# The first block's input projection as three split products, with the gates kept in DRAM

## The reference, cut to what matters

```python
x = layer_norm(x, ln_emb_g, ln_emb_b)
z = x @ w_in                                             # 1024 x 2048, with kr twice
xs, gs, cq, ckv, kr, gm = split(z)                       # 512, 512, 256, 128, 64, 512
ys = s5_branch(xs, ...) * silu(gs)                       # state-space scan, GELU, GLU
ym = mla_branch(cq, ckv, kr, ...) * silu(gm)             # latent attention, 4 heads
mix = concat([ys, ym]) @ w_out
```

## Time and profile before

| | |
|---|---|
| median of 3 runs | 2280.45 us (2280.33 to 2280.82) |
| profiled execution, first to last instruction | 2278.5 us |
| PE busy | 2194.5 us (96%) |
| DVE busy | 1154.4 us (51%) |
| POOL busy | 1192.3 us (52%) |
| ACT busy | 754.5 us (33%) |
| input projection and what lies between its tiles | 36.3 to 285.75 us |

### The profile page before, as it was taken

The page is one execution under the profiler, slowest core; times in us unless marked ns, Lnnn a source line. Parts: engine busy times, 40 slices in busy tenths (PEclk is TensorE's granted clock), DMA queues, the critical chain, the costliest instruction groups (busy, mean ns, idle before and its releaser), DMA issues.

```text
span 2278.5 us, 27616 instructions
## 1 busy us (share of the span) xinstructions
PE 2194.5 (96%) x10944; PEld 1609.4 (71%) x10944; DVE 1154.4 (51%) x1473; ACT 754.5 (33%) x1161; POOL 1192.3 (52%) x809
## 2 busy tenths in 40 slices
PE   6999999999999899999999999998999999999998
PEld 2454464676886687568866788876788888888886
DVE  6950844551186611550036724775966666652434
ACT  4121042332112511650036343135555555531211
POOL 2533510204787265435656765365688888844442
PEclk8999999999999999999999999999999999999999
DMA  3336232001223422101211235233122222154111
GB/s 134 111 74 104 84 85 70 4 19 47 92 84 98 143 65 84 34 10 37 89 25 51 83 111 194 87 144 130 47 62 82 83 82 84 64 182 157 47 37 74
DMA packets 62590, 187.73 MB, mean 82 GB/s; under 512 B 14903, under 2 KB 17255, under 8 KB 62415
## 3 DMA queue, kind: packets, MB, share of 16 engines
q1 hardware_dynamic: 50688, 143.30, 19.6%
q10 hardware_dynamic: 8688, 32.26, 3.8%
q0 software_dynamic: 3088, 10.43, 2.4%
HBM read 150.15 MB, written 33.59 MB: 81 GB/s over the span
## 4 chain that ended last, share of the span: by engine, by line
PE 89%; DVE 5%; ACT 3%; issue 2%; POOL 1%; DMA 1%; ACTq 0%; DVEq 0%
PE ps L3005 21%; PE ps L2651 16%; PE ps L2616 14%; PE ps L3124 10%; PE ps L2929 4%; PE ps L3038 3%; PE ps L325 3%; PE ps L3076 2%; PE ps L493 1%; PE ps L481 1%; PE ps L348 1%; PE ps L2731 1%; PE ps L607 1%; PE ps L618 1%; PE ps L630 1%
## 5 line engine op out<-in xcount | busy, mean ns | idle before, releaser
L1390 POOL TENSOR_TENSOR w_parts<-front,sb_zero 128x1024 fp32r<-128x1024 f32 x69 | 139.0, 2014 | 300.8 <-PE ps L3124 117.7
L3124 PE MATMUL ps<-ffn_parts,w_parts 128*128 128x512 f32 x1008 | 230.3, 389 | 1.5 <-DVE front L2577 1.5
L1463 POOL TENSOR_TENSOR up_parts<-front,up_parts 128x512 fp32r<-128x512 f32 x120 | 194.5, 1629 | 69.5 <-ACT up_parts L1736 69.5
L2616 PE MATMUL ps<-front 128*128 128x512 f32 x512 | 225.5, 599 | 2.7 <-ACT front L892 2.7
L1395 POOL TENSOR_TENSOR w_parts<-front,w_parts 128x1024 fp32r<-128x1024 f32 x75 | 207.6, 2769 | 22.5 <-ACT w_parts L1891 7.5
L3124 PEld LDWEIGHTS ps<-ffn_parts,w_parts 128*128 128x128 f32 x1008 | 189.0, 188 | 41.7 <-issue 2.6
L1300 POOL TENSOR_TENSOR front<-front,sb_csilu 128x1024 f32<-128x1024 f32 x48 | 104.3, 2172 | 210.5 <-DMA front<-w_ada 210.5
L3005 PE MATMUL ps<-t_high,up_parts 128*128 128x512 f32 x640 | 204.8, 391 | 4.9 <-ACT back L1743 4.9
L2651 PE MATMUL ps<-h_high,w_parts 128*128 128x512 f32 x672 | 187.6, 394 | 0.6 <-PE ps L2929 0.6
L2616 PEld LDWEIGHTS ps<-front 128*128 128x128 f32 x512 | 96.5, 191 | 118.6 <-issue 118.1
L3005 PE MATMUL ps<-h_high,up_parts 128*128 128x512 f32 x480 | 154.5, 389 | 1.5 <-DVE back L2345 1.5
(11 more groups left out here) (399 smaller groups left out, 4510.6 us busy)
## 6 DMA issues: line engine op xcount, KB each, us to landing
front<-w_ada SPq DMA_DIRECT2D x48, 512.0 KB, 3.6
front<-w_up SPq DMA_DIRECT2D x44, 512.0 KB, 4.4
front<-w_down SPq DMA_DIRECT2D x22, 512.0 KB, 3.6
front<-w_in SPq DMA_DIRECT2D x16, 512.0 KB, 3.6
front<-w_out SPq DMA_DIRECT2D x16, 512.0 KB, 4.7
residual<-back ACTq DMA_DIRECT2D x2, 4096.0 KB, 15.6
front<-w_gates SPq DMA_DIRECT2D x16, 512.0 KB, 4.0
gates<-back SPq DMA_DIRECT2D x16, 512.0 KB, 3.2
```

Source lines behind the costliest of these rows:

```text
L1390: pool.tensor_tensor(high, raw, zero[:, 0:1].to_broadcast((P, PAGE)), ALU.add)\
L1463: pool.tensor_tensor(parts[:, BANK:], src, parts[:, 0:BANK].bitcast(F32), ALU.subtract)\
L2616: mm = pe.matmul(ps[:, bank + nt, :], ring[:, slot, at + k * step:at + k * step + P], rhs(k0 + k)[:, nt * BANK:(nt + 1) * BANK], start=sta ...
L3124: mm = pe.matmul(ps[:, 2 * m + nt, :], parts[n % 2 + w_][:, at:at + P], half_of(AR[kk % 4 + x_], nt), start=k == 0 and q == 0, stop=k == N ...
```

## The change

1. `w_in` blocks and x are split. ACT copies each block's high part into one of eight pages (`win_high`); POOL subtracts it, and the low part takes the block's place in the ring (`win_low`). ACT makes x's high part `XH` (8 pages), DVE the low part `XL`, over x itself. A tile is then 48 float32r matmuls: low x XH first, which gives the ring slot back, then high x XH and high x XL. Tiles 0 and 1 go together: both parts x XH for each, then all of XL.
2. The pages for this come from the gates: `silu(gs)` and `silu(gm)` are written to DRAM one page at a time (ACT issues the write) and read back by POOL after the last tile. ACT waits for the writes that used pages 12, 13, 20 and 21 before it reuses them: before the chunk states are copied (L1559), those of the gates up to the tile just before.
3. The order of the tiles is 0 to 7, then `gm`'s four, then the latents. Two tiles (not four) stand before the chunk states and six (not four) behind them.
4. After the last tile POOL adds XL and XH back to x, eight operations, with the two read-backs between them.
5. The scan runs over two halves of the state, with half the scratch space: 24 operations of 1024 columns for the 12 of 2048, and the same 32 scans.
6. `GSB` is placed in `TM`'s rows, so `TM`'s clearing (L1308) moves from the kernel's start to behind tile 7, and DVE's scratch moves to pages 14 and 15. SP's loop of loads is unrolled with separate counts for w_in and w_ada. Several semaphores are merged into two.

```diff
+        IN_ORDER = (0, 1, 2, 3, 4, 5, 6, 7, 12, 13, 14, 15, 8, 9, 10, 11)
+        XH, XL = rounded_pages("x_high", (16, 17, 18, 19, 24, 25, 26, 27), FT), HH
...
@@ SP
+            for i in range(N_IN):
+                if i >= 2:
+                    sp.wait_ge(S("win_low_used"), i - 1)
+                load(2 * i, None, *tile_of(t["w_in"], IN_ORDER[i]))
+                if i >= 2:
+                    sp.wait_ge(S("ada_used"), i - 1)
+                load(2 * i + 1, None, *tile_of(t["w_ada"], i))
...
@@ POOL
+            def win_low(i):
+                pool.wait_ge(S("win_high"), i + 1)
+                pool.tensor_tensor(WIN_LOW[i], ring[:, 2 * i % RING, :], WIN_HIGH[i].bitcast(F32), ALU.subtract)\
+                    .then_inc(S("win_split"), 1)
...
+            for a in range(2):
+                ada_sum(a)
+            win_low(0)
+            win_low(1)
+            for i in (2, 3):
+                ada_sum(i)
+                win_low(i)
+            for i in range(4, 8):
+                win_low(i)
+                ada_sum(i)
+                if i == 6:
+                    pool.wait_ge(S("x_in_dram"), 16)
+                    pool.wait_ge(S("dve_step"), DVE_STEP["cp_table"])
+                if i >= 6:
+                    gather(2 * (i - 6))
+                    gather(2 * (i - 6) + 1)
+            pool.wait_ge(S("z_tile"), 8)
             pool.memset(TM, 0.0).then_inc(S("pool_step"), 1)
...
+            for i in range(8, N_IN):
+                win_low(i)
+                if i == 11:
+                    pool.wait_ge(S("pool_step"), POOL_STEP["tm_zero"])
+                    pool.wait_ge(S("dve_step"), DVE_STEP["g_skip"])
+                    for s in range(1, STEP):
+                        pool.dma_start(TM[s * GC:(s + 1) * GC, :, s * GC:P], GSB[:, :, 0:P - s * GC])\
+                            .then_inc(S("tm_landed"), 16)
+                ada_sum(i)
             pool.wait_ge(S("dve_step"), DVE_STEP["states_ready"])
             pool.dma_start(page(47).bitcast(I32), t["pos"].partition_broadcast(P)).then_inc(S("pos_landed"), 16)
-
-            ada_sum(15)
+            pool.wait_ge(S("z_tile"), N_IN)
+            for k in range(FT):
+                pool.tensor_tensor(XN[:, k, :], XL[k].bitcast(F32), XH[k].bitcast(F32), ALU.add)\
+                    .then_inc(S("x_whole"), 1)
+                if k % 4 == 3:
+                    pool.wait_ge(S("x_whole"), k + 1)
+                    pool.dma_start(GM if k > 4 else GS, silu_dram[k - 3:k + 1].rearrange("k p t -> p k t"))\
+                        .then_inc(S("gm_back" if k > 4 else "gs_back"), 16)
...
@@ ACT
+            win_high(0)
+            win_high(1)
+            for k in range(FT):
+                act.wait_ge(S("norm_scaled"), tiles_to("ln_emb", k + 1))
+                act.activation(XH[k], XN[:, k, :], ACT.Identity, bias=V("ln_emb_b", k)).then_inc(S("norm_ready"), 1)
...
+            def gate(tile):
+                n = tile - 4
+                at = page((12 if n < 4 else 20) + n % 2)
+                if n >= 2:
+                    act.wait_ge(S(f"gate_out{n % 2}"), 16 * (n // 2))
+                z(tile, at, ACT.Silu)
+                act.wait_ge(S("z_free"), tile + 1)
+                act.dma_start(silu_dram[n], at).then_inc(S(f"gate_out{n % 2}"), 16)
...
+            for tile in (8, 9):
+                gate(tile)
+                win_high(tile + 2)
+            act.wait_ge(S("gate_out0"), 16 * 3)
+            act.wait_ge(S("gate_out1"), 16 * 3)
+            act.wait_ge(S("dve_step"), DVE_STEP["tables_built"])
             for x in range(16, 24):      # copies of the chunk states
...
+            for tile in (10, 11):
+                gate(tile)
+                win_high(tile + 2)
+            act.wait_ge(S("gate_out0"), 16 * 4)
+            act.wait_ge(S("gate_out1"), 16 * 4)
             for tile in range(12, 16):
-                z(tile, GM[:, tile - 12, :], ACT.Silu)
+                z(tile, CQ[:, tile - 12, :] if tile < 14 else (CKV if tile == 14 else KR), ACT.Copy)
+                if tile < 14:
+                    win_high(tile + 2)
@@ DVE
+            for k in range(FT):
+                x = quarters(XN[:, k, :])
+                dve.scalar_tensor_tensor(x, x, V("ln_emb_g", k), SPREAD, ALU.mult, ALU.mult).then_inc(S("norm_scaled"), 1)
+            for k in range(FT):
+                dve.wait_ge(S("norm_ready"), tiles_to("ln_emb", k + 1))
+                dve.scalar_tensor_tensor(XL[k], XN[:, k, :], V("ln_emb_b", k), XH[k].bitcast(F32), ALU.add, ALU.subtract)\
+                    .then_inc(S("x_low"), 1)
...
+            for half in range(2):
+                qs = slice(half * PAIRS // 2, (half + 1) * PAIRS // 2)
+                tt(T1, s0, e1, ALU.mult)      # and the five others of each side, on half the pairs
+                for q in range(PAIRS // 2):   # two scans each
@@ PE
+            def in_first():
+                for i in range(2):
+                    pe.wait_ge(S("win_split"), i + 1)
+                    in_products(i, (WIN_HIGH[i], WIN_LOW[i]), (XH,), start=True, ready=None if i else
+                                lambda k: pe.wait_ge(S("norm_ready"), tiles_to("ln_emb", k + 1)))\
+                        .then_inc(S("win_low_used"), 1)
+                    if i == 0:
+                        ada_column(0, "ada_used")
+                        ada_column(1, "ada_used")
+                for k in range(FT):
+                    pe.wait_ge(S("x_low"), k + 1)
+                    for i in range(2):
+                        for nt in range(2):
+                            mm = pe.matmul(ps[:, 2 * i + nt, :], WIN_HIGH[i][:, k * P:(k + 1) * P],
+                                           XL[k][:, nt * BANK:(nt + 1) * BANK], start=False, stop=k == FT - 1)
+                        if k == FT - 1:
+                            mm.then_inc(S("z_tile"), 1)
+            def in_tile(i):
+                pe.wait_ge(S("win_split"), i + 1)
+                pe.wait_ge(S("z_free"), i - 1)
+                in_products(i, (WIN_LOW[i],), (XH,), start=True).then_inc(S("win_low_used"), 1)
+                in_products(i, (WIN_HIGH[i],), (XH, XL), stop=True, between=lambda: ada_column(i, "ada_used"))\
+                    .then_inc(S("z_tile"), 1)
```

More of the change, by code:

```diff
@@ L132, in program @@
         KR = page(23)
-        GSB = page(24, 4).rearrange("p (g n) -> p g n", g=GROUPS)
         GM = pages(24, 4)
@@ new lines, in _ @@
+            for i in range(4, 8):
[8 more added lines that the diff above has]
+            pool.wait_ge(S("z_tile"), 8)
+            pool.memset(TM, 0.0).then_inc(S("pool_step"), 1)
+            for s in range(4, STEP):
+                gather(s)
@@ L2662, in tile3, with in_products @@
                 return products(bank, WR[slot], WR[2 + slot], HH, HL, give_back, ready, between, step)
-            def with_ada(tiles, base, a0, done, free, rhs, ready=None):
-                for m in range(*tiles):
-                    b = base + 2 * m
-                    block_landed(b)
-                    if m >= 2:
-                        pe.wait_ge(S(free), m - 1)
-                    tile(2 * (m % 2), b % RING, rhs, ready=ready if m == 0 else None, give_back=m > 0,
-                         between=(lambda: ada_column(a0 + m - 1, "w_used")) if m else None).then_inc(S(done), 1)
+            def in_products(i, parts, inputs, start=False, stop=False, ready=None, between=None):
+                for k in range(FT):
+                    if ready:
+                        ready(k)
+                    if between and k == FT // 2:
+                        between()
+                    for n, (w_, x_) in enumerate((w_, x_) for x_ in inputs for w_ in parts):
+                        for nt in range(2):
+                            mm = pe.matmul(ps[:, 2 * (i % 2) + nt, :], w_[:, k * P:(k + 1) * P],
+                                           x_[k][:, nt * BANK:(nt + 1) * BANK], start=start and k == 0 and n == 0,
+                                           stop=stop and k == FT - 1 and n == len(parts) * len(inputs) - 1)
+                return mm
@@ L2678, in _ @@
             pe.wait_ge(S("act_step"), ACT_STEP["c_ready"])
-            xn = lambda k: XN[:, k, :]
-            with_ada((0, 8), 0, 0, "z_tile", "z_free", xn,
-                     lambda k: pe.wait_ge(S("norm_ready"), tiles_to("ln_emb", k + 1)))
+            in_first()
+            for i in range(2, 8):
+                in_tile(i)
             pe.wait_ge(S("dve_step"), DVE_STEP["w_table"])
@@ L2703, in _ @@
                 mm.then_inc(S("ssm_ps"), 1)
-            with_ada((8, 12), 0, 0, "z_tile", "z_free", xn)
+            for i in range(8, 10):
+                in_tile(i)
             pe.wait_ge(S("u_landed"), 16 * STEP)
@@ L2716, in _ @@
                 mm.then_inc(S("ssm_ps"), 1)
-            with_ada((12, 16), 0, 0, "z_tile", "z_free", xn)
+            for i in range(10, N_IN):
+                in_tile(i)
+            pe.sem_inc(S("w_used"), B_UKV)
```

(4 more changed lines are left out.)

219 lines of the change are left out of this document (119 added, 100 removed).

## The result

The changed kernel takes 2284.66 us (median of 19 runs, 2280.21 to 2285.96) beside 2280.62 for the kernel before on the same chip: a ratio of 1.0016, 95% interval 1.0009 to 1.0022. That is 4.0 us slower, and clear of noise; the forecast was 2258.2, 22.3 us faster, with a range of 2239 to 2270, so 26 us that were to be gained are missing. The profiled execution spans 2283.5 us (before: 2278.5), with a mean granted clock of 0.976 (before: 0.987).

A forecast was written before the change was run, and what follows sets the result against it. The prediction took PE to bound the first block up to the attention. It summed 3.1 + 39.8 - 0.6 - 3.8 = 38.5 us saved, less 16.2 of stalls behind the last tile, to 22.3 us gained: 2258.2 us, range 2239 to 2270.

The forecast's parts named there:

- Tiles 0 and 1: First two input tiles, run together with x split into XH and XL: 3.1 us saved.
- tiles 2 to 15: Input tiles as three split products, 11.12 us each instead of 13.96: 39.8 us saved.
- Behind tile 7: ACT late from a gate's DMA and two weight copies ahead of the table copies: 0.6 us lost, bounds 0 and 2.
- The chunk states: ACT may copy them only once tile 9's gate write has landed: 3.8 us lost, bounds 3.1 and 5.3.
- 0.70 us per us of POOL's work: DVE's loss per us of POOL's work beside it, read from the scan before and applied to the scan after.
- rival (c): POOL, slowed beside DVE's long operations, becomes the bound of the tiles: 2299 us; chance 0.05.
- The scan: DVE's scan in halves loses 20.8 us beside POOL, takes 61.6 and ends at T - 4.5.
- T: The end of the last tile, forecast 38.5 us earlier than before.
- Behind the last tile: Angles take 17.5 us beside POOL's additions, PE stalls 12.8; with a second stall 16.2 lost, bounds 0 and 25.1.
- no second one (3.4): Second PE stall behind the last tile, for the latent's norm and reciprocal on DVE: 3.4 us.
- rival (a): The scan ends early and nothing stalls behind the last tile: 2242.0 us; chance 0.26 for it or near it.
- the rule that the prediction had set aside: DVE and POOL share a port pair held per instruction, so each POOL us costs DVE one: 2267.1 us; chance 0.14.

The follow-up runs named there:

- the version with the order mended: Changed kernel with POOL's additions and gathers later, silu(c) multiplications of ada blocks 2 to 15 on ACT, and ACT's and POOL's order adjusted: 2242.44 us.
- the run with the gathers later: Changed kernel with POOL's wait for cp_table and four gathers moved behind tile 7's low part and ada sum: 2284.58 us, 1.0025 of the kernel before.
- the run without the sums: Changed kernel with POOL's ada sums of tiles 2 to 15 replaced by 8-column copies (part of the computation left out): 2273.67 us.
- The run without POOL's sums and with its additions later: Changed kernel with ada sums of tiles 2 to 15 replaced by 8-column copies and POOL's eight additions moved behind the y gathers: 2240.19 us.
- the run in which PE was kept busy: Changed kernel with useless multiplications filling PE's three waits (ahead of tile 7, at the chunk states, at the outputs): 2278.91 us, 0.9999 of the kernel before.
- the doubling: Kernel before with one more POOL operation of 128 x 1024 on each of ada blocks 0 to 15, doubling the block: 2288.51 us, 1.0047.
- additions later: Changed kernel with POOL's eight additions of XL and XH moved from behind the last tile to behind the y gathers: 2265.55 us, 0.9932.
- The small-tables run: Changed kernel with POOL's ada sums of tiles 2 and 3 held back until DVE has its small tables: 2284.82 us, 1.0027 of the kernel before.

## Why the prediction was wrong

The measured time lies outside the range and on the side that had been given a chance of 0.05. By the prediction's own steps, from tile 0's start (35.37; before 36.31):

- Tiles 0 and 1, tiles 2 to 15: right. Both tiles and their copies took 61.47 - 35.37 = 26.1 us, where tile 1 ended at 65.9 before, 29.6 after the start: 3.5 saved (forecast 3.1). Then 11.12 a tile, 39.8 saved.
- Behind tile 7: 17.7 us against 17.0 in the kernel before, 0.7 lost (0.6).
- **The chunk states: wrong, and with them what stands ahead of tile 7.** The step priced ACT's wait for tile 9's gate and no other. That wait exists: in the version with the order mended PE waits 2.6 us for it and the chunk states take 11.7 us, 4.4 lost where 3.8 was forecast. In the changed kernel DVE's tables were later: 10.4 us ahead of tile 7, 1.5 for its first part at the low clock (5.25 instead of 3.79), and 17.8 us for the states instead of 7.3, so 10.5 lost and not 3.8. The last tile ended 19.6 us earlier and not 38.5 (these terms give 20.2; 0.6 isn't assigned).
- **The term left out** is the stretch of the tables. The prediction read DVE's rows from 230 us on and carried their 0.70 us per us of POOL's work to the scan, but never asked it of the 103 us of tables ahead; only its rival (c) looked at them, for POOL's lateness and not DVE's. They ended 77.1 us before the chunk states (145.5 and 222.56, the latter in the earlier trace rows). Of these the change takes 27.9 by moving the states two tiles up, 26.4 by what PE saves until there, 9.1 by XL's operations and 35.0 by POOL's work: late by 21.3, and 20.7 is the wait that the run with the gathers later shows in one piece. With the prediction's own rate, 0.70 x 40 = 28 in place of the 35, they would still have been some 14 us late.
- The scan: right. It took 63.0 us (61.6), so 22.2 us were lost beside POOL (20.8), and ended 3.2 us before T (4.5).
- Behind the last tile: right in mechanism, too small in size. The angles took 290.76 - 267.38 = 23.4 us (17.5), because three one-input operations took 2.72 each and the three of 1.25 took 13.37 together, where 1.25 had been added to each. The stall was 19.2 (12.8). There was no second one (3.4), as the additions were over at 286.4, before the sines; in the run without the sums, where they weren't, it came and was 9.5 us. The low clock, which the prediction had at nothing, took another 3.3 in the group behind the stall (7.5 us instead of 4.2) and 5.0 up to the outputs' end. T to the outputs' end is 60.8 us instead of 36.6: 24.2 lost and not 16.2.

Together 18.9 + 8.0 = 26.9 us against the forecast, and the outputs end 4.6 us later, counted from tile 0, where 22.3 earlier had been expected. Of the rivals, (c), POOL as the bound, had the sign right, and the mark it gave for itself, PE idle ahead of a tile and released by POOL, was seen once. Its mechanism didn't happen: that wait was POOL's own wait for DVE, and moving it gained nothing.

What was bought and where it went: the saved 43 us of PE's work were real. The run without POOL's sums and with its additions later shows 40 of them (2240.2; forecast of rival (a) 2242.0), and the version with the order mended, which computes everything, 38 (2242.4). In the changed kernel DVE became the bound, so that a faster PE is worth nothing up to 293 us; that is shown by the run in which PE was kept busy.

Shown is that POOL's work beside DVE stretches the tables and the angles: it was taken away, added and moved, and DVE followed each time. What stays open is how much a us of POOL's work costs DVE. From before to after it is 35 / 40 = 0.87, with the doubling 9.4 / 10.2 = 0.92, but from the run without sums to the mended version 14.6 / 36.3 = 0.40. POOL's busy time is itself stretched by DVE, and the kind of operation differs (the mended version's POOL has no multiplication); no run separates the two. The amount alone doesn't set it: without the sums POOL was busy for 38.8 us and the tables took 105.3, in the kernel before for 45.6, and they took 102.7.

## What to carry to other kernels

When a change makes the bounding engine faster, list for every other engine the whole stretch between its fixed points, not only the place that is nearly late today: 77 us of slack were used up by a stage moved up (28), PE's own savings (26), new work (9) and a collision (35). Here each us of POOL's work beside DVE's tables cost DVE 0.4 to 0.9 us. Moving such work in time gained where it landed beside a DVE that had time (the additions) and nothing where it didn't (the small tables); moving a part of it to a third engine shortened the tables. And count a wait of PE as its length plus what PE does afterwards at half the clock: here a wait of 9.5 us cost 21 more.

## What the hardware showed

What a wait of PE costs in clock doesn't go by its length. Behind 19.2 us of standing still (after) the clock was back after 11 us of work, and all nineteen executions lie between 2280.2 and 2286.0. Behind 9.5 us (no sums), 3.6 (additions later) and 1.9 (the kernel before with more of POOL's work) it stayed at 1.2 GHz for 45 to 55 us with PE busy in 10.00 of every 10 us. Of the latter two these are the profiled executions, and others of the same kernels were about 20 us faster; without the sums all ten lay between 2271.5 and 2275.5 us. The small-tables run had both behind its 19.5 us: two executions, the profiled one among them, took 2303.4 and 2304.3 us, the eight others 2281.5 to 2286.0. With the gathers later, one of ten took 2303.9. The work in this stretch is multiplications of 128 columns in float32; it kept a high clock when it began with one, for 36 us on end. The Trainium skill (TensorE: Matmul & The Clock Gate, Part 1: The HAM clock gate) has the clock set by how busy PE has lately been; the fall agrees. Why a PE that is busy without a gap isn't given its clock back for 45 us, and in other executions of the same kernel is, no run here shows.

DVE's operations with one input of 1024 columns (0.69 to 0.75 us alone) took 2.72 us three times beside POOL's additions, which took 10.62 / 4 = 2.66 each, and once 9.79. The Trainium skill (SBUF — State Buffer, Who interferes with whom) says that in the two-port modes whoever issues first holds the shared pair for the whole instruction and the other blocks; the 2.72 agree with one addition each, and the 9.79 is as long as four of them in a row (9.23), which one held instruction doesn't explain. It is near the rule that the prediction had set aside for the 0.70 of operations with two inputs.
